# Weights split in place in a ring of 12, a residual quarter by a trip through DRAM, and mixer steps ahead of splits

## The reference

```python
for i in range(2):
    hn = rms_norm(h, norm_mix[i])
    mix = gla_mixer(hn, ...) if i == 0 else diff_attn_mixer(hn, pos, ...)
    h = h + mix
    h = h + swiglu(rms_norm(h, norm_ffn[i]), ffn_w_in[i], ffn_w_out[i])
    gate = sigmoid(rms_norm(h, ple_norm[i]) @ ple_w_gate[i])
    h = h + gate * (p[i] @ ple_w_proj[i])
```

```python
la_f = log_sigmoid(zf @ w_gate_f + b_gate_f) / 16      # and la_b
b = cumsum(log_a, axis=3)
q_in = qf * exp(b)
scores = einsum(q_in, kf * exp(-b))
```

## Time and profile before

| | us |
|---|---|
| median of three timed runs | 898.88 (898.36 to 898.9) |
| profiled execution, its own time | 899.7 |
| its span | 897.9 |
| PE busy in it | 892.8 (99%) |
| DVE busy | 653.1 (73%) |
| ACT busy | 506.9 (56%) |
| DMA to HBM and back | 208 GB/s over the span |

### The profile page before, as it was taken

The page is one execution under the profiler, slowest core; times in us unless marked ns, Lnnn a source line. Parts: engine busy times, 40 slices in busy tenths (PEclk is TensorE's granted clock), DMA queues, the critical chain, the costliest instruction groups (busy, mean ns, idle before and its releaser), DMA issues.

```text
span 897.9 us, 12240 instructions
## 1 busy us (share of the span) xinstructions
PE 892.8 (99%) x4364; PEld 738.6 (82%) x4364; DVE 653.1 (73%) x985; ACT 506.9 (56%) x820; POOL 69.4 (8%) x88
## 2 busy tenths in 40 slices
PE   9999999999999999999999999999999999999998
PEld 8988888888888888778888888888888888887777
DVE  5985478777745688997787777645778997779763
ACT  6756455444444666788664444434665555577681
POOL 0000100000000303211000000000010000215100
PEclk9999999999999999999999999999999999999999
DMA  7674558867755656434387766746567876566621
GB/s 258 205 236 136 179 186 293 283 235 240 247 202 187 226 187 221 143 116 141 127 277 268 244 243 237 253 137 235 197 244 239 286 248 211 191 212 226 222 87 47
DMA packets 76988, 187.47 MB, mean 209 GB/s; under 512 B 6852, under 2 KB 31812, under 8 KB 76936
## 3 DMA queue, kind: packets, MB, share of 16 engines
q1 hardware_dynamic: 75480, 182.99, 59.9%
q0 software_dynamic: 1024, 3.15, 1.0%
q10 hardware_dynamic: 432, 0.66, 0.2%
HBM read 171.83 MB, written 14.94 MB: 208 GB/s over the span
## 4 chain that ended last, share of the span: by engine, by line
PE 98%; DMA 1%; DVE 1%; ACT 0%; issue 0%; DVEq 0%; ACTq 0%
PE bank L1818 86%; PE bank L1856 3%; PE bank L1871 1%; PE bank L2131 1%; PE bank L2157 1%; PE bank L2241 1%; PE bank L2271 1%; DMA h_land<-gate_blocks 1%; PE bank L2142 0%; PE bank L1914 0%; PE bank L1978 0%; PE bank L2227 0%; PE bank L2026 0%; PE bank L2030 0%; PE bank L2251 0%; PE bank L2117 0%
## 5 line engine op out<-in xcount | busy, mean ns | idle before, releaser
L699 ACT ACTIVATE whi<-raw 128x1024 fp32r<-128x1024 f32 x295 | 306.3, 1060 | 181.2 <-DMA raw<-stream_dram 106.2
L1108 DVE TENSOR_TENSOR wlo<-raw,whi 128x1024 fp32r<-128x1024 f32 x295 | 347.9, 1214 | 57.1 <-ACT whi L699 56.7
L1818 PE MATMUL bank<-whi,x_hi 128*128 128x512 f32 x560 | 152.5, 394 | 0.0
L1818 PE MATMUL bank<-wlo,x_hi 128*128 128x512 f32 x560 | 149.9, 390 | 0.0
L1818 PE MATMUL bank<-whi,x_lo 128*128 128x512 f32 x560 | 149.8, 389 | 0.0
L1818 PEld LDWEIGHTS bank<-wlo,x_hi 128*128 128x128 f32 x560 | 105.2, 188 | 22.1
L1818 PEld LDWEIGHTS bank<-whi,x_lo 128*128 128x128 f32 x560 | 105.2, 188 | 21.9
L1818 PEld LDWEIGHTS bank<-whi,x_hi 128*128 128x128 f32 x560 | 103.6, 188 | 22.1 <-issue 1.8
L1818 PE MATMUL bank<-whi,y_hi 128*128 128x512 f32 x396 | 107.8, 394 | 0.6 <-ACT ple_gate L895 0.5
L1818 PE MATMUL bank<-wlo,y_hi 128*128 128x512 f32 x396 | 106.0, 390 | 0.0
L1818 PE MATMUL bank<-whi,y_lo 128*128 128x512 f32 x396 | 106.0, 390 | 0.0
(11 more groups left out here) (252 smaller groups left out, 898.7 us busy)
## 6 DMA issues: line engine op xcount, KB each, us to landing
raw<-stream_dram SPq DMA_DIRECT2D x295, 512.0 KB, 4.6
ffn_blocks<-ffn_blk SPq DMA_DIRECT2D x22, 256.0 KB, 2.0
ffn_land<-ffn_blocks SPq DMA_DIRECT2D x22, 256.0 KB, 4.0
second_blocks<-h_blk SPq DMA_DIRECT2D x8, 256.0 KB, 2.0
h_land<-second_blocks SPq DMA_DIRECT2D x8, 256.0 KB, 2.8
cv_blocks<-cv_blk SPq DMA_DIRECT2D x7, 256.0 KB, 5.0
cv_land<-cv_blocks SPq DMA_DIRECT2D x7, 256.0 KB, 3.1
h_blocks<-h_blk SPq DMA_DIRECT2D x3, 512.0 KB, 6.3
```

The costliest lines, as they stand in the source:

```text
L699: A(whi[:, u % RING, :], raw[:, u % RAW, :], ACT.Copy).then_inc(sem("w_hi"), 1)
L1108: V.tensor_tensor(wlo[:, u % RING, :], raw[:, u % RAW, :], whi[:, u % RING, :].bitcast(F32), ALU.subtract).then_inc(sem("w_lo"), 1)
L1818: last = T.matmul(bank[pair + t][:, :], lhs[a][:, kt, t * P:(t + 1) * P], w[:, u % RING, kk * NW:(kk + 1) * NW], start=part != 1 and k == ...
```

## The change

- `raw` and `wlo` become one buffer of 12 slots: DVE writes `wlo` over `raw`. A load of unit n from 12 on waits for `w_used` to reach n - 11 and for the landing of unit n - 4, not for DVE. `whi` stays a ring of 8.
- Trips by `second_blocks` and `gate_blocks` become one function, `trips`, with names in `PIECES`. They stand three loads further back in SP's order (`half_blocks` two; the convolution's and its middle three).
- In each PLE, columns 768 to 1023 of the residual take a trip of their own (`ple0 q1`, `ple1 q1`), so that PE transposes four blocks where it did eight. The five first units of the PLE go by `GATE_ORDER`, the projection's third. The first sigmoid waits for both tiles, and DVE's gated products wait for one sigmoid each. A small sigmoid into `spare` stands ahead, so that the table is loaded there. The second gate product goes to banks 4 and 5 (`pair=4`).
- `GLA_ORDER`: on ACT `expabs` from 6 to 5 and `ln` from 7 to 5; on DVE `gates` from 5 to 4. `DF_ORDER`: on DVE `more` 1 and `unit` 1 from 10 to 8 and 9.
- The loops are written out.

```diff
-RAW, RING = 4, 8
+PACE, SLOTS, RING = 4, 12, 8
+GATE_ORDER = ((0, 0), (0, 1), (1, 0), (0, 2), (0, 3))
...
-        (6, "expabs", 0), (7, "ln", 0), (9, "cumulate", 0), (10, "cumulate", 1), (13, "tile", 3), (17, "cross", 0),
+        (5, "expabs", 0), (5, "ln", 0), (9, "cumulate", 0), (10, "cumulate", 1), (13, "tile", 3), (17, "cross", 0),
...
-        (4, "zT", 0), (4, "tile", 1), (5, "z4", 0), (5, "gates", 0), (7, "ln", 0), (9, "tile", 2),
+        (4, "zT", 0), (4, "tile", 1), (5, "z4", 0), (4, "gates", 0), (7, "ln", 0), (9, "tile", 2),
...
                 for n in range(lo, hi):
-                    sp.wait_ge(sem("w_lo"), max(n - RAW + 1, 2))
-                    sp.dma_start(raw[:, n % RAW, :], stream[SOURCE[n]]).then_inc(sem(f"raw{n % RAW}"), 16)
+                    if n < SLOTS:
+                        sp.wait_ge(sem("w_lo"), max(n - PACE + 1, 2))
+                    else:
+                        sp.wait_ge(sem("w_used"), n - SLOTS + 1)
+                        sp.wait_ge(sem(f"raw{n % PACE}"), 16 * (n // PACE))
+                    sp.dma_start(raw[:, n % SLOTS, :], stream[SOURCE[n]]).then_inc(sem(f"raw{n % PACE}"), 16)
...
-            def gate_blocks(n, tile):
-                at = END[tile + 2] + 8
+                done = trips(END[tin + FT + 2] + 11, f"ple{n} q1")
+                done = trips(END[tin + FT + 4] + 11, f"gate{n} t0", f"gate{n} t1")
...
 -                lhs_hi(src, norm_gain(j), (6, 7))
+                lhs_hi(src, norm_gain(j), (6,))
                 squares(j, 1)
+                split_to(END[tple] + 8)
+                pair_hi(j, src, f"ple{n} q1", 6)
+                A(spare[:, n:n + 1], cols[:, 0:1], ACT.Sigmoid)
...
-                        A(sig[:, k, :], bank[2 * (t % 2) + k][:, :], ACT.Sigmoid, scale=rstd[:, j, k:k + 1])\
+                        A(sig[:, k, :], bank[(4 if half else 2 * (t % 2)) + k][:, :], ACT.Sigmoid, scale=rstd[:, j, k:k + 1])\
...
 -                    V.tensor_tensor(wlo[:, u % RING, :], raw[:, u % RAW, :],
+                    V.tensor_tensor(wlo[:, u % SLOTS, :], raw[:, u % SLOTS, :],
                                     whi[:, u % RING, :].bitcast(F32), ALU.subtract).then_inc(sem("w_lo"), 1)
...
 -                residual(tout + 1, 1)
+                for lo in (HALF // 2, 0):
+                    for t in range(TT):
+                        V.tensor_tensor(h[:, t, HALF + lo:HALF + lo + HALF // 2], h[:, t, HALF + lo:HALF + lo + HALF // 2],
+                                        bank[2 * ((tout + 1) % 2) + t][:, lo:lo + HALF // 2], ALU.add)\
+                            .then_inc(sem("h_part" if lo else "h_new"), 1)
+                    if lo:
+                        dve.wait_ge(sem("h_part"), TT * (n + 1))
+                        pair_blk(f"ple{n} q1", 0, 6, False)
...
-                    dve.wait_ge(sem("ple_sig"), TT * (2 * n + half + 1))
                     for k in range(TT):
+                        dve.wait_ge(sem("ple_sig"), TT * (2 * n + half) + k + 1)
                         V.tensor_tensor(gated[:, k, :], sig[:, k, :], bank[2 * ((t + 1) % 2) + k][:, :], ALU.mult)\
...
 -                product(tple, src, "ple_sig", need=more2, hooks=[(1, second_half2)])
-                product(tple + 1, PT, "ple_gated", need=[("pT", 2 * (n + 1))])
+                for at, (t, k) in enumerate(GATE_ORDER):
+                    if at == 2:
+                        pe.wait_ge(sem("h_new"), 4 * (3 * n + 1) + 4)
+                        more2[2:3] = lhs_T(h, (6,))
+                    product(tple + t, PT if t else src, "ple_gated" if t else "ple_sig" if k == 3 else None,
+                            need=[("pT", 2 * (n + 1))] if t else more2, only=k, at=END[tple] + at)
...
-                product(tple + 2, src, "ple_sig")
+                product(tple + 2, src, "ple_sig", pair=4)
```

More of the change, by code:

```diff
@@ L77, with piece, slot, turn @@
 LAST = ((0, 0, NW), (1, 0, NW // 2), (1, NW // 2, NW))
+PIECES = ("mix0 q0", "mix0 q1", "ple0 q1", "gate0 t0", "gate0 t1", "mix1 q0", "mix1 q1", "ple1 q1", "gate1 t0", "gate1 t1",
+          "cv q0", "cv q1", "mb q0", "mb q1")
+GATE_ORDER = ((0, 0), (0, 1), (1, 0), (0, 2), (0, 3))
 PAIR_ORDER = ((0, 0), (0, 1), (1, 0), (1, 1), (0, 2), (0, 3), (1, 2), (1, 3))
+def piece(name):
+    return PIECES.index(name)
+def slot(name):
+    return int(name[-1])
+def turn(name):
+    return sum(slot(other) == slot(name) for other in PIECES[:piece(name) + 1])
 def done_at(tile):
@@ L225, in wait @@
     def wait(self, eng, name, value):
-        if self.turn is not None:
-            eng.wait_ge(self.sem(name), self.turn * self.rate[name] + value)
-        elif value > 0:
+        if value > 0:
             eng.wait_ge(self.sem(name), value)
[L231 to L239, removed]
 def build(nc, stream, x, p, cols_d, rows_d, consts_d, wgate_d, out):
@@ L889, in ffn @@
                     t = tple + 2 * half
-                    split_to(END[t + 1] + AHEAD - 2 * half)
-                    c.wait(act, "w_used", END[t + 1])
+                    over = END[t + 1 + (half == 0)]
+                    split_to(over + AHEAD - 1 - half)
+                    c.wait(act, "w_used", over)
                     if half:
@@ L1378, in ffn @@
                     parts(t - 1, 2 * (t - 1 - tin), END[t + 1] + (3 if t == tin + 1 else 1))
[L1379 to L1388 removed]
+                for t in range(tin + 3, tin + FT):
                     product(t)
@@ L1645, in _ @@
                 conv_parts(t - 1, t - 1 - CV_IN, END[t + 1] + (3 if t == CV_IN + 1 else 1))
[L1646 to L1654 removed]
+            for t in range(CV_IN + 3, CV_IN + 7):
+                conv_product(t)
+                conv_blocks(t)
+                conv_parts(t - 1, t - 1 - CV_IN, END[t + 1] + 1)
             conv_product(CV_IN + 7)
@@ L1762, in _, with place @@
             free = {}
+            def place(w, u):
+                return u % (RING if w is whi else SLOTS)
             def claim(b):
@@ L2070, in ffn @@
                 other = Y if src is X else X
-                first_tiles(tin, src, "ffn_mid", list(got) + second_need(2 * n))
+                first_tiles(tin, src, "ffn_mid", list(got) + second_need(f"mix{n}"))
                 product(tin + 2, src, "ffn_mid")
-                turns = (FT - 5) // 2
-                with pe.Fori(0, turns) as i:
-                    c.enter(i, {"w_hi": 8, "w_lo": 8, "w_used": 8, "ffn_mid": 4})
-                    for t in (tin + 3, tin + 4):
-                        product(t, src, "ffn_mid")
-                    c.leave(turns)
-                for b, (name, value) in list(free.items()):
-                    free[b] = (name, value + (turns - 1) * {"ffn_mid": 4}.get(name, 0))
-                for t in range(tin + 3 + 2 * turns, tin + FT):
+                for t in range(tin + 3, tin + FT):
                     product(t, src, "ffn_mid")
@@ L2197, in cv_T @@
                 free[b] = ("cv_lhs", 8)
-            first_tiles(CV_IN, X, "cv_prod", list(half) + second_need(4))
+            first_tiles(CV_IN, X, "cv_prod", list(half) + second_need("cv"))
             product(CV_IN + 2, X, "cv_prod")
-            with pe.Fori(0, 2) as i:
-                c.enter(i, {"w_hi": 8, "w_lo": 8, "w_used": 8, "cv_prod": 4})
-                for t in (CV_IN + 3, CV_IN + 4):
-                    product(t, X, "cv_prod")
-                c.leave(2)
-            for b, (name, value) in list(free.items()):
-                free[b] = (name, value + {"cv_prod": 4}.get(name, 0))
+            for t in range(CV_IN + 3, CV_IN + 7):
+                product(t, X, "cv_prod")
             product(CV_IN + 7, X, "cv_prod")
```

256 lines of the change are left out of this document (106 added, 150 removed).

## The result

| | before | after |
|---|---|---|
| median, us | 898.88 | 901.27 |
| lowest to highest of nine | 898.36 to 900.28 | 900.88 to 904.28 |
| profiled execution | 899.7 | 900.88 |
| its span | 897.9 | 899.1 |

The changed kernel is slower: the ratio is 1.0034, with a 95% interval of 1.0025 to 1.0043. The time lies in the forecast range (898.6 to 902.0), 0.8 us over the point (900.5), on the far side of the 0.2% border: the prediction gave 42% to that and 51% to no change. Its nine executions are of two kinds that have to be told apart. Five have a mean granted clock of 1.000 and took 900.88 to 901.27. Four have 0.998 and took 902.51 to 904.28. The profile is of the first kind.

What follows compares the result with a forecast made beforehand. PE, 98% of the chain, was taken to bound the kernel, never held up by weights. Gates +2.63, transposes -0.43, first PLE's end -0.60 gave +1.60 on 898.88: 900.5 us, range 898.6 to 902.0.

Steps and rivals of the forecast that it cites:

- 0.2% border: Smallest difference told from no change, 0.2% or 1.8 us: borders 897.1 and 900.7 us.
- The gate chain: First mixer's gates: L1309 waits for the late copy and subtraction, delaying PE's cumulating matmuls and L2011; +2.63, ends 2.4 and 2.9.
- The transposes: Each PLE: half of PE's eight residual transposes go through DRAM instead; -0.43 per layer, -0.87 in all.
- The second gate product's banks: First PLE's end: other banks spare PE the second sigmoid's wait (0.47); gain 0.6 including 0.43 from transposes, ends 0.1 and 0.9.
- The wait of 0.3 to 0.6 for h: Sign of being right: PE waits for h at transposes one unit later, replacing the sigmoid wait.
- the differences hold for either: Claim that predicted differences apply both to the profiled execution (899.7) and to the timed median (898.88).
- The written-out loops and the ring: Loops: 0, since "issue" has 0% of the chain; 12-slot ring with split in place and later trips: 0, from -0.2 to +0.3.
- The moved trips: Trips three loads later in SP's order: issued as early as before; 0, from -0.2 to +0.3 together with ring and split.
- The argument that PE waits for no split: Earlier loads and shorter copy waits gain nothing, since PE's list of waits has no split; taken as 0.
- The clock: Rival: PE's clock falls to 1.2 GHz in the new pause, 2.72 more per unit, one unit gives 903.2; 3%.

Runs made afterwards that it cites:

- the kernel with the old banks: Changed kernel with DVE's step behind the logarithms at 6 instead of 7, plus the second gate product in its former banks: 902.55 us, ratio 1.0046.
- the new table alone: Kernel before with only the changed kernel's GLA_ORDER on ACT and DVE: 902.87 us, ratio 1.0050 (five executions); run again for a trace, 902.28.
- the changed kernel with the old table: Changed kernel with the GLA_ORDER of the kernel before on ACT and DVE: 898.28 us, ratio 0.9997.
- padding: Changed kernel with the former GLA_ORDER and 16 or 64 more already fulfilled waits on SP ahead of the last loads: 897.93 (ratio 0.9989) and 898.07 us.

## Why the prediction was right, and what it missed

**The gate chain** was the largest term, +2.63, with PE waiting 2.3 to 2.4. The trace has 2.32, and 2.70 up to L2002 (from 0.72 ahead to 1.98 behind). Each step stands as it was put: exponentials, table, logarithms, copy, subtraction, L1297, and DVE's delay arriving whole at L2002 since DVE has no slack there. The gates did start 0.7 sooner than in the earlier trace rows, but so did PE's products for them, so it is no gain of the table's. (The unit that the prediction calls 11 is number 12 in the code's count, in which 0 are the gates' small weights.)

**The transposes**, -0.43 in each layer: -0.40 in each (PE goes from 1.96 to 1.56 behind in the first, from 1.05 to 0.65 in the second). Right.

**The second gate product's banks**: the forecast was a gain of 0.17 beyond the transposes, with a landing of 4.58. In the changed kernel's trace PE goes from 1.56 to 0.93 behind, so the whole delay of 0.63 is gone. The wait of 0.3 to 0.6 for h, which was to stand in its place one unit later, did not come, since ACT waited for the first landing alone; the second was there when ACT came to it (eight copies in a row):

```profile
325.53 2.68 ACT L890 ACTIVATE y_hi<-h_land,cols 128x128 fp32r<-128x128 f32 x8 [3.02 <-DMA h_land<-residual_blocks]
```

Here the prediction's mechanism is wrong. The sigmoid behind these copies ends at 329.36, before PE is due at 329.99, so PE would not have waited in the old banks either; the kernel with the old banks shows no wait there. What went away is a slow landing: the second took 2.67 here. And that wait is not a fixed property of the kernel before: in three traces of kernels whose PLE is unchanged PE is held 0.25 and 0.22 (the new table alone, twice) and not at all (the loops written out):

```profile
327.91 1.07 PE L1778 MATMUL bank<-whi,y_hi 128*128 128x512 f32 x4
```

The step that failed is taking a wait for a landing from one execution, which lay 0.8 above the median, and subtracting it from the median: "the differences hold for either" is wrong where the difference is a wait that comes and goes. The 0.17 lies within what these traces show, 0 to 0.63, by luck.

**What was taken at zero.** The written-out loops and the ring were put at 0 since "issue" has 0% of the chain. Half a us behind the last matmul goes with the place of a block of SP's program, which these two most likely moved, and the loops alone cost 1.5 in the kernel before; in the changed kernel with the old table, which has them and the ring, nothing of the 1.5 shows. The moved trips, put at 0, are 0. The argument that PE waits for no split was too short: in the written-out kernel a late load held ACT's copy, behind it stood a step of the mixer, and that is what PE waited for.

**The clock** was a rival at 3%, priced at 2.7 for a unit. It decides in four of nine executions and costs 1.6 by the medians. The argument against it was that no pause of PE as long as that was in the trace, which says nothing about a pause of 2.3, and that the start has 1.00 throughout, which is misread. The first record of the clock in that trace begins at 7.35 us; before it there is none, and the view shows 1.00 for want of one. PE's matmuls of 128x256 start 0.43 apart up to there and 0.22 apart in the same place of a trace whose record begins at 4.86 (last section): the pace of the low level, after an idle start. So the trace did hold a sign that the clock is low when PE has been idle. The Trainium skill ("TensorE: Matmul & The Clock Gate", Part 1: The HAM clock gate) says that an idle array is put to half its clock; the second run of the new table alone agrees, with 0.50 from 45.20 to 48.40. That the median still lies in the forecast range is partly luck: five of nine executions kept the clock (with the new table alone one of five did), and had one more lost it, the median would be about 902.5, beyond the range.

**The sum.** With the terms as measured, for executions at 1.000: +2.7 for the gates, +0.5 for SP's outputs and +0.1 in the second mixer, less 0.8 for the transposes, make 2.5, less a wait that is 0 to 0.6 from execution to execution. The five executions lie 2.2 above the median of before (901.08 against 898.88), the four with the clock's fall 1.6 higher. The point was 0.8 low: 0.5 for SP's outputs, 0.2 for the second kind of executions, which move the median, and 0.1 for the gates and the transposes. The upper end of the forecast (901.3) left out the +0.3 and +0.2 that the prediction itself allowed to terms put at 0, though its lower end has such a -0.2; with them it would be 901.8.

## What to carry to other kernels

Where an engine does its work strictly in order, moving a step ahead of a copy puts everything that needs the copy behind the step: follow the moved-over instruction, here one copy of 1 us, to who waits for it on the other engines. A wait of the busiest engine costs more than its length if its clock falls afterwards (here 1.6 more by the medians), so look at the clock of several executions, not at one profile. And a wait for a landing that one profile shows should be looked for in a second before it is counted as a gain.

## What the runs showed of the hardware

- In kernels with a pause of PE of 2.3 us the granted clock fell in 9 of 15 executions. In the one such trace it did not fall at once: PE ran about 1.5 us at full clock first, then at half of it (1.2 instead of 2.4 GHz) up to 48.4. After pauses of 1.4 (the kernel with the old banks, five executions) it did not fall. Without either, one of 11 executions of the written-out loops has the same mean clock, 0.998.
- In the first microseconds matmuls take up to twice as long, and when that ends differs from execution to execution: in each of the 12 traces at the time at which its first record of the clock begins, from 4.09 to 7.35 us. The 1.00 that the views show before it is no measurement. The same matmuls in the kernel before (record from 7.35 on) and in the one with the new table alone (from 4.86 on):

```profile
5.09 1.09 PE L1871 MATMUL bank<-consts,h 128*128 128x128 f32 x4
5.97 1.72 PE L1924 MATMUL bank<-gla_r 128*128 128x256 f32 x4
```

```profile
5.00 0.63 PE L1871 MATMUL bank<-consts,h 128*128 128x128 f32 x4
5.46 1.03 PE L1924 MATMUL bank<-gla_r 128*128 128x256 f32 x4
```

  That moves the whole rest by up to 0.9 us (the one with the new table alone is 0.87 ahead at 20 us), so two traces must be compared behind that point.
- Where a fetch of a block of SP's program (8 KB) falls while the last output is under way, the kernel ends some 0.5 us later; where padding moved it away, both were gone.
